# Where a block-triangular inverse is started: TensorE levels 1 to 4, or VectorE with the blocks moved through memory

## The reference

```python
A = jnp.where(strict, jnp.einsum('nbhid,nbhjd->nbhij', kb, k) * decay, 0.0)
rhs = jnp.concatenate([v * beta[..., None], kb * jnp.exp(gc)[..., None]], -1)
sol = lax.linalg.triangular_solve(jnp.eye(C, dtype=jnp.float32) + A, rhs,
                                  left_side=True, lower=True, unit_diagonal=True)
```

## Time and profile before

| | |
|---|---|
| Time, median of 3 runs | 2701.13 us (2700.47 to 2702.29) |
| The profiled execution | 2700.57 us, of which the trace's span is 2698.8 us |
| TensorE busy | 2646.1 us, 98% |
| VectorE / ScalarE / GpSimd busy | 1380.5 / 1148.0 / 226.6 us |
| Mean granted TensorE clock | 0.993 of 2.4 GHz |

### The profile page before, as it was taken

The page is one execution under the profiler, slowest core; times in us unless marked ns, Lnnn a source line. Parts: engine busy times, 40 slices in busy tenths (PEclk is TensorE's granted clock), DMA queues, the critical chain, the costliest instruction groups (busy, mean ns, idle before and its releaser), DMA issues.

```text
span 2698.8 us, 40360 instructions
## 1 busy us (share of the span) xinstructions
PE 2646.1 (98%) x16806; PEld 2361.4 (87%) x16806; DVE 1380.5 (51%) x2175; ACT 1148.0 (43%) x1977; POOL 226.6 (8%) x367
## 2 busy tenths in 40 slices
PE   7999999999999999999999999999999999999998
PEld 5789888788888788899999998998877797999998
DVE  4746664654555465634444456535554447354344
ACT  5554446554545245433333345434332344332334
POOL 5011101100001001110000001110000000000000
PEclk8999999999999999999999999999999999999999
DMA  6554324523323345543333335554434334233222
GB/s 187 160 141 111 96 80 133 155 77 90 98 74 102 86 130 173 176 143 102 106 94 98 103 95 169 167 150 125 125 118 125 118 107 131 90 106 110 91 90 81
DMA packets 367317, 318.13 MB, mean 118 GB/s; under 512 B 11417, under 2 KB 339155, under 8 KB 367136
## 3 DMA queue, kind: packets, MB, share of 16 engines
q1 hardware_dynamic: 336224, 207.91, 26.7%
q0 software_dynamic: 30912, 107.64, 13.0%
HBM read 260.54 MB, written 54.96 MB: 117 GB/s over the span
## 4 chain that ended last, share of the span: by engine, by line
PE 81%; DVE 4%; ACT 3%; issue 1%; POOLq 0%; POOL 0%; ACTq 0%; DVEq 0%
PE dense L554 71%; PE mixer L554 8%; DVE wlo L1586 1%; ACT arena L1075 1%; PE mixer L794 1%; ACT whi L1075 1%; DVE hf L1724 0%; DVE hlo L1720 0%; ACT relu L1075 0%; PE mixer L996 0%; PE mixer L924 0%; DVE accA L1661 0%; ACT hhi L1075 0%; PE mixer L945 0%; ACT h1hi L1075 0%
## 5 line engine op out<-in xcount | busy, mean ns | idle before, releaser
L554 PE MATMUL dense<-hhi,whi 128*128 128x272 f32 (+1 forms) x3072 | 853.4, 332 | 16.9 <-DVE hlo L1720 8.4
L554 PE MATMUL dense<-hlo,whi 128*128 128x272 f32 (+1 forms) x3072 | 825.7, 323 | 0.0
L554 PE MATMUL dense<-hhi,wlo 128*128 128x272 f32 (+1 forms) x3072 | 825.6, 323 | 0.0
L1586 DVE TENSOR_TENSOR wlo<-wst,whi 128x1024 fp32r<-128x1024 f32 x384 | 469.6, 1223 | 237.6 <-ACT whi L1075 236.8
L554 PEld LDWEIGHTS dense<-hhi,whi 128*128 128x128 f32 x3072 | 515.5, 189 | 76.0 <-issue 15.1
L1075 ACT ACTIVATE whi<-wst 128x1024 fp32r<-128x1024 f32 x384 | 403.8, 1051 | 388.8 <-PE dense L554 383.4
L554 PEld LDWEIGHTS dense<-hhi,wlo 128*128 128x128 f32 x3072 | 514.8, 189 | 42.7
L554 PEld LDWEIGHTS dense<-hlo,whi 128*128 128x128 f32 x3072 | 517.1, 189 | 36.7 <-issue 0.7
L554 PE MATMUL dense<-h1hi,whi 128*128 128x272 f32 (+1 forms) x1536 | 426.3, 332 | 10.3 <-DVE wlo L1586 6.1
L554 PE MATMUL dense<-h1hi,wlo 128*128 128x272 f32 (+1 forms) x1536 | 415.3, 324 | 0.0
L554 PE MATMUL dense<-h1lo,whi 128*128 128x272 f32 (+1 forms) x1536 | 415.1, 324 | 0.0
(11 more groups left out here) (333 smaller groups left out, 1828.7 us busy)
## 6 DMA issues: line engine op xcount, KB each, us to landing
wst<-in_w_ff_dram SPq DMA_DIRECT2D x256, 512.0 KB, 3.9
wst<-in_w_in_even_dram SPq DMA_DIRECT2D x48, 512.0 KB, 4.0
wst<-in_w_in_odd_dram SPq DMA_DIRECT2D x48, 512.0 KB, 3.9
proj<-ffh POOLq DMA_DIRECT2D x48, 272.0 KB, 2.5
proj<-ffh POOLq DMA_DIRECT2D x48, 256.0 KB, 2.3
arena<-proj POOLq DMA_DIRECT2D x16, 512.0 KB, 5.1
wst<-in_w_out_even_dram SPq DMA_DIRECT2D x16, 512.0 KB, 4.1
arena<-proj POOLq DMA_DIRECT2D x8, 1024.0 KB, 8.1
```

What stands on the lines that cost most here:

```text
L554: return pe.matmul(out, lhsT, rhs, start=start, stop=stop)
L1586: TT(wlo[:, u % 2, :], wst[:, u % 2, :], whi[:, u % 2, :].bitcast(F32), ALU.subtract)\
```

## The change

For tiles 0 to 7 the levels 0 to 2 (blocks of 1, 2 and 4 to blocks of 8) leave TensorE. A now carries a minus sign (the negated beta is kept in `cols`), so subtractions become additions. GpSimd stores A (four heads, 128x128) to memory at kk, waits for it, and loads the 64 diagonal blocks of 8x8 back, one in each of 64 partitions (`C`). VectorE inverts them at b1 with ten small instructions in all (a memset, four 2-wide multiplications and additions, two 4x4 products of a multiplication and a reduction each, and at b3 a transposing copy to `CT`). GpSimd stores C and CT to the diagonals of a matrix in memory that was zeroed at the start, waits, and loads all of it, 128x1024 values, to XX (Xi and XiT). TensorE's first level is q = 3. For q = 3 and 4 the transposes that the next level needs are made by VectorE in 32x32 squares after lb; only q = 6 keeps the TensorE transposes and ScalarE's copies. The sample tile keeps its way. GpSimd's multiplication moves from dec to vT. In the side list the entries l0 and la, lb for q = 1 and 2 go; one rest, b1, b2 (empty here), b3 and three rests come between vT and la for q = 3. For scale, the side lists grow from 84 to 90 entries on the 69 rows, and from 147 to 155 on the 244 rows. The final wait of SyncE's queue uses one semaphore in place of two.

```diff
+LB = 3
+WB = 1 << LB
+CB = WB * WB + WB
+NL = LEVELS - LB
...
-            out += [("g", t, s, 0) for s in ("vT", "l0")]
+            out.append(("g", t, "vT", 0))
             more = i + 1 < len(tiles)
             if more:
                 out.append(("gx", t + 1))
-            for q in range(1, LEVELS):
+            out += [("rest",)] * 1 + [("g", t, s, 0) for s in ("b1", "b2", "b3")] + [("rest",)] * 3
+            for q in range(LB, LEVELS):
...
+            if n == P:
+                sq, t2 = (m[k].rearrange("p h n -> p (h n)") for k in ("SQ", "RB"))
+                m["C"], m["CT"], m["U"] = carve(sq[0:NBLK], (CB,), (WB * WB,), (WB * WB // 4,))
+                m["tmp"] = t2[0:NBLK, 0:512]
...
+        arow = nc.dram_tensor("arow", (H, P * (P + 1)), F32)
+        xrow = nc.dram_tensor("xrow", (2 * H, P * (P + 1)), F32)
+
+        def by_token(rows):
+
+            return rows[:, 0:P * P].rearrange("h (t n) -> t h n", n=P)
+
+        def diagonal(rows):
+
+            v = rows.rearrange("h (b x) -> (h b) x", x=WB * (P + 1))[:, 0:WB * P]
+            return v.rearrange("b (i n) -> b i n", n=P)[:, :, 0:WB]
@@ tensor: la, lb
-                        w("inv", base + 2 * q - 1 + p)
+                        if q == LB:
+                            w("bin", 32 * (t + 1))
+                            if p:
+                                w("ru")
+                        else:
+                            w("inv", inv_at(t, q - 1, p))
                         for h in (2 * p, 2 * p + 1):
                             last = mm(M4(3 * p)[0:r, h % 2, 0:r], m["A"][0:n, h, 0:r], m["XiT"](h)[:, c0:n])
                         s(last, "t2")
-                        if q > 1:
+                        if q == LEVELS - 1:
...
-                        if q > 1:
-                            w("xi", basei + 2 * q - 3 + p)
+                        w("t2s", t2_at(t, q, p))
+                        if q == LEVELS - 1:
+                            w("xi", 2 * t + p + 1)
@@ scalar: act, la
-                        w("A", t)
+                        w("bout", 48 * t + 16)
...
-                elif step == "la" and q > 1:
+                elif step == "la" and q == LEVELS - 1:
@@ vector
+            def product(m, out, left, right, b):
+
+                tmp = m["tmp"][:, 0:b ** 3].rearrange("p (i c j) -> p i c j", i=b, c=b)
+                link(TT(tmp, left.unsqueeze(2).broadcast_to([NBLK, b, b, b]),
+                        right.rearrange("p j c -> p c j").unsqueeze(1).broadcast_to([NBLK, b, b, b]), ALU.mult))
+                link(dve.tensor_reduce(out, tmp, mybir.AxisListType.X, ALU.add))
...
+                elif step == "b1":
+                    w("bin", 32 * t + 16)
+                    dve.memset(m["C"][:, 0:CB:WB + 1], 1.0)
+                    v = m["C"].rearrange("p (s x) -> p s x", x=4 * WB + 4)[:, :, 0:4 * WB]
+                    v = v.rearrange("p s (i w) -> p s i w", w=WB)
+                    k = WB // 4
+                    tmp = m["tmp"][:, 0:2 * k].rearrange("p (s i) -> p s i", s=k)
+                    for row, into, x in ((v[:, :, 2:4, 1], v[:, :, 2:4, 0], v[:, :, 1, 0]),
+                                         (v[:, :, 2, 0:2], v[:, :, 3, 0:2], v[:, :, 3, 2])):
+                        link(TT(tmp, row, bcl(x, [NBLK, k, 2]), ALU.mult))
+                        link(TT(into, into, tmp, ALU.add))
+                    for s_ in range(WB // 8):
+                        merge_left(m, 8 * s_, 4)
+                        merge_right(m, 8 * s_, 4)
+                elif step == "b2" and LB == 4:
+                    merge_left(m, 0, 8)
+                elif step == "b3":
+                    if LB == 4:
+                        merge_right(m, 0, 8)
+                    c = m["C"][:, 0:WB * WB].rearrange("p (i j) -> p i j", j=WB)
+                    s(dve.tensor_copy(m["CT"].rearrange("p (j i) -> p i j", i=WB), c), "inv")
...
+                    if LB <= q < LEVELS - 2:
+                        for p in range(2):
+                            w("inv", inv_at(t, q, p))
+                            dve.transpose(m["XX"][:, 0, 2 * p:2 * p + 2], m["XX"][:, 1, 2 * p:2 * p + 2])
@@ gpsimd: constants, then gdn
+                dma(by_token(xrow[:, :]), lmask[:, 0:1, :].broadcast_to([P, 2 * H, P]))\
+                    .then_inc(S("g_bout"), 16)
...
+                pool.wait_ge(S("g_bout"), 16)
...
+            def base_blocks(t, name):
+                m = gdn_map(t)
+                if name == "kk":
+                    pool.wait_ge(S("g_A"), t + 1)
+                    dma(by_token(arow[:, :]), m["A"]).then_inc(S("g_bout"), 16)
+                    pool.wait_ge(S("g_bout"), 48 * t + 32)
+                    dma(m["C"][:, 0:WB * WB].rearrange("p (i j) -> p i j", i=WB), diagonal(arow[:, :]))\
+                        .then_inc(S("g_bin"), 16)
+                else:
+                    pool.wait_ge(S("g_inv"), t * (1 + 2 * NL) + 1)
+                    for a, k in enumerate(("C", "CT")):
+                        dma(diagonal(xrow[a * H:(a + 1) * H, :]), m[k][:, 0:WB * WB].rearrange("p (i j) -> p i j", i=WB))\
+                            .then_inc(S("g_bout"), 16)
+                    pool.wait_ge(S("g_bout"), 48 * t + 64)
+                    dma(m["XX"].rearrange("p a h n -> p (a h) n"), by_token(xrow[:, :])).then_inc(S("g_bin"), 16)
+
             def gdn(t, name, q):
-                if name == "dec":
+                if t < TILES and name in ("kk", "b3"):
+                    base_blocks(t, name)
+                elif name == "vT":
```

More of the change, by code:

```diff
@@ L409, in build, with inv_at, t2_at, x_at @@
         GROWS = relu2[0:H, 1, :]
+        NBLK = P // WB * H
+        def inv_at(t, q, p):
+            return t * (1 + 2 * NL) + (2 * (q - LB) + p + 2 if t < TILES else 2 * q + p + 1)
+        def t2_at(t, q, p):
+            return t * 2 * NL + 2 * (q - LB if t < TILES else q) + p + 1
+        def x_at(t, q, p):
+            return t * 2 * NL + 2 * (q - LB if t < TILES else q - 1) + p + 1
         def gdn_map(t):
@@ L546, in _ @@
             sp.wait_ge(S("y_dve"), 7)
[L547 to L549 removed]
+            sp.dma_start(y_sample.rearrange("b s d -> (b s) d"), ystage[0:NS, 4, :]).then_inc(S("y_last"), 16)
+            sp.wait_ge(S("y_last"), 16 * 9)
         @block.tensor
@@ L796, in gdn @@
                 elif step == "lb":
-                    if q == 1:
+                    if q in (1, LB):
                         w("qk")
@@ L808, in gdn @@
                 elif step == "zw":
-                    w("inv", base + 2 * lv)
+                    w("inv", inv_at(t, lv - 1, 1))
                     if n == NS:
@@ L1798, in gdn_prep, with block_of, merge_left, merge_right @@
                         dve.memset(St, 0.0).then_inc(S("g_state"), 1)
+            def block_of(m, i0, j0, b):
+                return m["C"][:, 0:WB * WB].rearrange("p (i j) -> p i j", j=WB)[:, i0:i0 + b, j0:j0 + b]
+            def product(m, out, left, right, b):
[3 more added lines that the diff above has]
+                link(dve.tensor_reduce(out, tmp, mybir.AxisListType.X, ALU.add))
+            def merge_left(m, o, b):
+                u = m["U"][:, 0:b * b].rearrange("p (i c) -> p i c", i=b)
+                product(m, u, block_of(m, o + b, o, b), block_of(m, o, o, b), b)
+            def merge_right(m, o, b):
+                u = m["U"][:, 0:b * b].rearrange("p (i c) -> p i c", i=b)
+                product(m, block_of(m, o + b, o, b), block_of(m, o + b, o + b, b), u, b)
             def gdn(t, step, q):
@@ L1828, in gdn @@
                     for h in range(H):
-                        last = STT(m["A"][0:n, h], M4(0)[0:n, h, 0:n], beta[:, h:h + 1], m["Dm"][0:n, h],
+                        last = STT(m["A"][0:n, h], M4(0)[0:n, h, 0:n], nbeta[:, h:h + 1], m["Dm"][0:n, h],
                                    ALU.mult, ALU.mult)
@@ L1850, in gdn @@
                     for p in range(2):
-                        w("t2s", base + 1 + p)
-                        s(TT(m["XX"][0:n, p, 2:4], bcm(ident[0:n, 0:n], [n, 2, n]), m["T2"][0:n, 2 * p:2 * p + 2],
-                             ALU.subtract), "inv")
+                        w("t2s", t2_at(t, 0, p))
+                        s(TT(m["XX"][0:n, 1, 2 * p:2 * p + 2], m["T2"][0:n, 2 * p:2 * p + 2],
+                             bcm(ident[0:n, 0:n], [n, 2, n]), ALU.add), "inv")
                 elif step == "la":
                     for p in range(2):
-                        w("t2", base + 2 * q + 1 + p)
+                        w("t2", t2_at(t, q, p))
                         r, c0 = half(q, n)
```

35 lines of the change are left out of this document (16 added, 19 removed).

## The result

| | before | after |
|---|---|---|
| Median | 2702.29 us (5 runs, 2700.47 to 2702.93) | 2712.23 us (5 runs, 2712.15 to 2716.47) |
| Span of the profiled execution | 2698.8 us | 2710.4 us |
| Mean granted clock of TensorE | 0.993 | 0.986 |

The ratio is 1.0043, 95% interval 1.0032 to 1.0053: 10 us slower, where 2691 us, 10 us faster, was predicted. The lines of after are shifted: the matmul helper is L587 (L554 before), ScalarE's L1075 is L1112, VectorE's wlo L1586 is L1623.

The account below looks back on a forecast made before the run. TensorE's queue was taken to bound the kernel. Removed work -48.2, waits in tiles 0 to 3 +26.9, tiles 4 to 7 +1, clock +10.4 gave -9.9 us on 2700.6: median 2691 us, range 2660 to 2710.

Parts of the forecast that it names:

- The records (416): TensorE's instruction records were to fall by 8 x 52 = 416.
- the removed work: Products and transposes leaving TensorE in eight tiles: 45.7 us, or 48.2 us gained with two waits of 2.5 us.
- The waits of the tiles 0 to 3: TensorE standing at la of q = 3 for XX: 5.2, 7.7, 7.7 and 6.3 us, together 26.9.
- the way of A: Serial chain from A through memory and VectorE to XX: 17.8 us, ends 15 and 25; 21.3 with delays in tile 1.
- The cover: Time from A to la's place that TensorE fills with other work: 13.6 us in tile 1.
- I count 1 us in all for the tiles 4 to 7: Waits for XX in the MLP's 244 rows: 8.7 us from b3 to la against 9.3 of stores and load.
- The clock: TensorE's clock falls behind four waits of 5 to 8 us, 2.6 us each: 10.4 us.
- rival (c): Denser side list puts la and lb together more often: six more places, 5 us, 2696 us; chance 0.13.
- (b): 32 B pieces make C and CT transfers 5 us slower, tiles 4 to 7 wait too: 2733 us; chance 0.17.
- (a): The way of A is hidden and TensorE never stands at la: 2653 us, near case 2661 or 2669; chance 0.25.

Follow-up runs that it names:

- no_way: Changed kernel without the transfers and block inversion, XX being a copy of the identity at b3 (wrong output): 2659.04 us, ratio 0.984 to the kernel before.
- more_rests: Changed kernel with eight rests in place of three between b3 and la of q = 3, tiles 4 to 7 only: 2691.77 us, ratio 0.9963 to the kernel before.
- copy_early: Changed kernel with VectorE's copy to CT and its signal moved from b3 to the end of b1: 2696.82 us, ratio 0.9985 to the kernel before.
- few_weights: Changed kernel with the layer 0 group 0 MLP's weight DMAs bringing only an eighth or a quarter: 2705.43 us, ratio 1.0014 to the kernel before.
- gx_late: Changed kernel with the next tile's gx loads moved behind b3 in the side list, same number of entries: 2706.97 us, ratio 1.0023 to the kernel before.
- late_tiles: Changed kernel with levels 0 to 2 back on TensorE for tiles 0 to 3, memory way with eight rests for tiles 4 to 7: 2670.23 us, ratio 0.9884.
- split_load: Changed kernel storing CT first and loading XiT alone for la, with Xi loaded after C for lb: 2686.07 us, ratio 0.9942 to the kernel before.
- fill: Changed kernel with eight rests in tiles 4 to 7, plus 24 useless fp32 products ahead of la's wait in tiles 0, 1 and 3: 2689.16 us, ratio 0.9955.

## Why the prediction was wrong

**Right.** The records (416), the removed work, and with it most of the gain: `no_way` is 42.2 us faster than the kernel before beside it, where 48.2 was said. Its busy time is 48.5 lower, where 45.7 was worked out. VectorE's ten instructions take 2.0 us in tile 0 (2.3 taken), and the store of A is 3.0 there as taken.

**Right by luck.** The waits of the tiles 0 to 3 are 27.1 against 26.9, but tile by tile they are 7.3, 8.4, 3.1 and 8.2 against 5.2, 7.7, 7.7 and 6.3. A is made by these instructions of VectorE:

```profile
161.94 1.13 DVE L1887 SCALAR_TENSOR_TENSOR arena<-mixer,cols,arena 128x128 f32<-128x128 f32 x4 [2.95 <-ACT arena L1112]
...
229.54 1.12 DVE L1887 SCALAR_TENSOR_TENSOR arena<-mixer,cols,arena 128x128 f32<-128x128 f32 x4
...
294.10 1.12 DVE L1887 SCALAR_TENSOR_TENSOR arena<-mixer,cols,arena 128x128 f32<-128x128 f32 x4
...
354.36 1.12 DVE L1887 SCALAR_TENSOR_TENSOR arena<-mixer,cols,arena 128x128 f32<-128x128 f32 x4
```

From the end of each row to the start of la the way of A took 22.8, 22.3, 21.9 and 21.5 us, 88.5 together, where 20.3, 21.3, 21.3 and 18.8 were taken, 81.7. The cover, from the same ends to la's place (its start less the wait), was 15.5, 13.9, 18.7 and 13.3 us, 61.4 together, where 15.1, 13.6, 13.6 and 12.5 were taken, 54.8. The way was 6.8 us longer and the cover 6.6, 5.1 of it in tile 2, and these two errors cancel. In the way, C lands 3.3 to 4.1 us behind the issue of its load (2.8 taken), and in tile 0 the store of a projection holds GpSimd up for 1.9 us.

**The step that failed** is the count for the second half: "I count 1 us in all for the tiles 4 to 7". It was 10.5 us. Tile 4 has each part in the rows above. The prediction had 8.7 us of cover against 9.3 of way, a wait of 0.6. The cover was 545.7 - 538.6 = 7.1, so 1.6 less: VectorE did not come to b3 early, as the prediction allowed, but 2.2 us after b1 had ended, because the plan puts a split that waits for ScalarE between them. The way was 11.8: stores 4.9 where 3.8 was taken (1.1), load 6.4 where 5.1 was (1.3), hand-overs 0.5 (0.1). 0.6 + 1.6 + 1.1 + 1.3 + 0.1 = 4.7. With no reserve left, each of these three went straight into the wait, and each was tried: `more_rests` gives the cover back and takes all of it away, `copy_early` moves the start and takes 8.6 of the 10.5 (in part because the stores ran quicker), `few_weights` takes the traffic and 5.5. The tiles 5 and 6 are of the same kind: stores and load took 11.0 and 10.8 us there, where 8.9 was taken; in tile 7, which does not wait, 7.9.

**The clock** is the second term that was too small, in number and not in size. Behind every wait for XX of 3.1 us and more the windows show 0.50: six falls, where four were counted. Busy time over that of `no_way` is 15.1 us (experiment 1), 2.5 for each of the six, since the fall behind the wait of 3.4 us for VectorE is in both. The two falls that went in `copy_early` gave back 4.5, about 2.2 each; 2.6 was taken. In all 4.7 us more than the 10.4.

**The sum again**, on the profiled executions. The span was to fall by 9.9 us and rose by 11.6 (2698.8 to 2710.4), 21.5 apart. Of these, 9.7 are more waits for XX, 4.7 more of the clock, 6.6 are gain that is missing without the way too (41.6 between the spans of before and `no_way`, where 48.2 was said), and 0.5 other idle time. The 6.6 is rival (c), which had put 5 us on the new order, near in size but not in form: the pieces are one wait of 3.4 us and longer waits for wlo and hlo, not six of up to 0.9. The waits and the clock alone, 14.4 us, turn the sign; the waits alone would have brought the gain to nothing.

**The rivals.** (b) put the slow side on the pieces of 32 B. Its form was right, since the reserve of the tiles 4 to 7 was what broke. Its cause was not seen where little else moves: two stores need 3.2 us there (tile 7, and tile 0 of `gx_late`), less than the 3.8 taken. In the tiles 4 to 6 of after they need 4.7 to 5.3, and there it stays open whether the pieces have a part in it, since without 512 of them the store took 2.5 and 1.9 us less in the tiles 4 and 6, and almost as long in tile 5. The Trainium skill (DMA: Bandwidth & Descriptors, Where the ~2 us actually goes) has a fixed cost of about 2 us in each transfer; 2.4 us for a single store in a quiet stretch agrees, and the loads of 512 KB, 4.8 us at the median even in `few_weights`, are above the estimated 3.2 of that fit. (a) is what `late_tiles` and `more_rests` show for the tiles 4 to 7, once five entries are given to it, and `no_way`'s 2659 is what the whole would be worth if all were hidden.

**Open.** Why the stores take 4.0 to 4.5 us in the tiles 4 to 6 even with the weights' traffic cut, and a single one 5.2 in tile 5, when tile 7 has 3.1 and 2.4. The same two stores take 3.1 to 6.1 us in the tiles 3 to 7 of the runs above, and no run separates what else is under way there.

## What to carry to other kernels

Work that leaves the bounding engine by way of memory is worth what its latency leaves over, and that is to be counted stage by stage, from the place where the last engine in the order lets the transfer start to the place of the first use. When such a sum comes out within a microsecond of zero, it is no hidden stage but an unknown one: two of the three extra waits here brought the clock's fall with them, over 2 us on top. Give the chain more entries of the order, let it start the moment its data is there, split the transfer so that the first use waits for its own half, and where a stage has no room (tiles 0 to 3) leave the work where it was.

## What was not expected of the hardware

- The place of one 0.2 us copy in VectorE's queue was worth 15 us. The waits of the tiles 4 and 6 all but went, and two falls of the clock with them; part of it was quicker stores.
- The length of a wait does not settle whether the clock falls. It fell behind every wait for XX of 2.6 us and more, and also behind one of 1.7 us (tile 2 of `split_load`, 0.51 in the window 312 to 314), one of 2.0 (tile 2 of `gx_late`, 0.50 in the window 314 to 316) and one of 2.0 that followed 24 products (`fill`). It did not behind those of 0.9 (`copy_early`), 1.6 (after) and 2.2 us (`few_weights`).
- A second store of 512 pieces of 32 B on the same queue added only 0.7 us to the 2.4 of the first in tile 7. Elsewhere the same two took up to 6.15 us (tile 0, behind 1.3 MB of loads).
- VectorE's transposes in 32x32 squares, whose price no row of before showed, take 0.40 to 0.44 us for 128x256 values in fp32 (0.77 for two in a row in tile 5 of after), nearer the low end of the bounds taken (0.17 and 1.12).
